# A decoder layer's way into its expert stage: the first two searches, the samples' mixing and four weight loads set in another order

## What is computed

```python
x = x + (ga * ya + gb * yb) @ w_out
x = x + peer(rmsnorm(x, norm_ffn), peer_wq, peer_keys, peer_u, peer_v)

def peer(tb, wq, keys, u, v):                      # 8 heads, 128 keys in each half
    q = (tb @ wq).reshape(blk, 8, 256)
    s1 = einsum('thd,hkd->thk', q[..., :128], keys[:, 0])
    s2 = einsum('thd,hkd->thk', q[..., 128:], keys[:, 1])
    sc1, i1 = top_k(s1, 16)
    sc2, i2 = top_k(s2, 16)
    cand = sc1[..., :, None] + sc2[..., None, :]   # 16 x 16 sums
    sc, sel = top_k(cand, 16)                      # 16 experts of 16384
    idx = (i1 * 128 + i2) at sel
    g = softmax(sc)
    act = gelu(einsum('thkd,td->thk', u[idx], tb))
    return einsum('thk,thkd->td', g * act, v[idx])
```

## Time and profile before

| | us |
|---|---|
| median of 3 runs | 2117.23 |
| lowest, highest | 2110.43, 2120.0 |
| profiled execution | 2117.6 |
| its span, first to last instruction | 2116.1 |
| its mean granted TensorE clock | 0.824 |
| TensorE matmul, VectorE, ScalarE, GpSimd busy | 1670.0, 1447.7, 489.1, 667.8 |
| transfers | 749.11 MB, mean 354 GB/s |
| gathers | 528, median 12.8 from issue to landing |

### The profile page before, as it was taken

One profiled execution on the slowest core, in us unless ns is written; L12 is line 12 of the kernel. 1 busy time (PEld: TensorE's weight loads), 2 busy tenths in 40 slices (PEclk: granted clock), 3 DMA queues, 4 the chain that ended last, 5 costly groups with the idle time before them and its releaser, 6 DMA issues. The chain is left out here.

```text
span 2116.1 us, 30101 instructions
## 1 busy us (share of the span) xinstructions
PE 1670.0 (79%) x10874; PEld 842.1 (40%) x10874; DVE 1447.7 (68%) x3666; ACT 489.1 (23%) x1413; POOL 667.8 (32%) x614
## 2 busy tenths in 40 slices
PE   7999999877777666666789999997777866666666
PEld 6887677433333111111168786773332421111111
DVE  3557533778778878877726575347877878887786
ACT  2246211211121221111223553122121112111112
POOL 0011000444554454444300110004454444444442
PEclk9999999877897676665799999999787876666658
DMA  5458895999999999999854688969999999999997
GB/s 205 157 204 305 300 389 229 387 370 420 416 421 421 404 416 420 421 415 414 366 181 150 218 318 297 387 240 408 404 421 420 416 420 402 421 421 420 416 413 304
DMA packets 135936, 749.11 MB, mean 354 GB/s; under 512 B 16611, under 2 KB 17100, under 8 KB 57298
## 3 DMA queue, kind: packets, MB, share of 16 engines
q0 software_dynamic: 84640, 588.54, 68.2%
q1 hardware_dynamic: 51138, 158.55, 20.6%
HBM read 735.70 MB, written 11.52 MB: 353 GB/s over the span
## 5 line engine op out<-in xcount | busy, mean ns | idle before, releaser
L1221 PE MATMUL ps<-arena 64*64 64x512 f32 x4096 | 753.2, 836 | 384.0 <-DVE arena L1841 381.7
L2463 POOL DMA_INDIRECT arena<-in_peer_uv,arena x528 | 619.9, 1174 | 792.2 <-PE ps L1221 642.7
L1832 DVE CUSTOM_DVE_ANT_0 arena<-arena,h 128x1024 f32<-128x1024 f32 x512 | 627.3, 1225 | 241.3 <-DMA arena<-in_peer_uv,arena 235.4
L1221 PEld LDWEIGHTS ps<-arena 64*64 64x64 f32 x4096 | 141.1, 166 | 938.6 <-DVE arena L1841 889.7
L573 PE MATMUL ps<-ht_tok,wring 128*128 128x264 f32 (+1 forms) x1536 | 362.9, 395 | 4.5 <-DMA wring<-in_w_in 3.1
L2204 ACT ACTIVATE arena<-arena 128x1 f32<-128x1 f32 x528 | 105.4, 203 | 975.1 <-DVE arena L1832 974.0
L573 PEld LDWEIGHTS ps<-ht_tok,wring 128*128 128x128 f32 x1536 | 292.8, 194 | 75.6 <-issue 19.9
L1841 DVE TENSOR_SCALAR arena<-consts,arena 128x64 f32<-128x64 f32 (+1 forms) x528 | 164.6, 312 | 25.2 <-ACT arena L2204 24.6
L573 PE MATMUL ps<-arena,wring 128*128 128x264 f32 x256 | 64.1, 393 | 2.7 <-DVE arena L1536 2.7
L573 PE MATMUL ps<-arena,gate 128*128 128x256 f32 x256 | 59.0, 382 | 0.0
L2440 POOL DMA_DIRECT2D nrow<-in_norm_ffn x2 | 1.1, 536 | 174.2 <-PE ps L925 174.2
(11 more groups left out here) (374 smaller groups left out, 1791.3 us busy)
## 6 DMA issues: line engine op xcount, KB each, us to landing
arena<-in_pages SPq DMA_DIRECT2D x256, 272.0 KB, 6.1
wring<-in_w_in SPq DMA_DIRECT2D x36, 1024.0 KB, 5.0
arena<-in_peer_uv,arena POOLq DMA_INDIRECT x528, 12.8
h<-in_state_ssm POOLq DMA_DIRECT2D x16, 512.0 KB, 6.1
out<-h POOLq DMA_DIRECT2D x16, 512.0 KB, 6.3
wring<-in_w_ssm_proj SPq DMA_DIRECT2D x8, 1024.0 KB, 10.8
arena<-in_w_out SPq DMA_DIRECT2D x8, 1024.0 KB, 9.4
wring<-in_peer_wq SPq DMA_DIRECT2D x8, 1024.0 KB, 9.7
```

Of the source, the lines that this page charges most:

```text
L1221: last = pe.matmul(ps[to:to + 64, SUM_BANK[t] + i, :], diag[rows, n % DIAGS, 0:64], ring[rows, HOME[n % RING], cols], start=n in TILE_FIRS ...
L1832: dve.tensor_tensor_reduce(ring[:, HOME[k], 0:D_MODEL], ring[:, HOME[k], 0:D_MODEL], tokens, 1.0, 0.0, ALU.mult, ALU.add, dots[:, column(n ...
L2463: pool.indirect_dma_start(ring[:, HOME[k], :], None, table, bass.IndirectOffsetOnAxis(ap=idx[:, TOPK * u + j:TOPK * u + j + 1], axis=0)).t ...
```

## The change

- TensorE's order: the four products of tile 0 come first; the samples' mixing and its turns stand behind the fourth, among the turns of tile 0's normed rows; `sample_heads`, `sample_mla_parts` and `sample_mla` stand behind scores 0; queries and scores of head 1 stand behind `out(3, 1)`, directly ahead of the outputs.
- Norm of tile 0 in parts: ScalarE squares each quarter when it is added, and the rows are scaled in two halves, each of which is turned by itself. The first query product starts on the first half.
- Corner search: for heads 0 and 1 of tile 0 the first eight numbers are searched among the 8 x 8 sums of the best eight of either half, the second eight among all 16 x 16. Both hand over eight numbers at a time. No piece of head 1's search stands ahead of the slots; in slots 5 to 8 four pieces run each.
- Tiles 1 and 2: squares, root and norm two slots later; TensorE's turns behind outputs 8, 9 and 10, head 2's products behind 12 and 13, its scores behind 14 as before.
- Loads: heads 0, 3 and 4 when the newest sample's scores are made, head 2 into the rear half of `gate` when tile 0 and 1 are mixed, heads 1, 5 and 6 behind `sample_mla_parts`, head 7 as before. To make the room of head 0's block free early, ScalarE copies the samples' latents aside. Rooms in the arena are in another order, and the rows of `peer_wq` are laid so that the turns read contiguous columns.

```diff
     for first in range(3):
-        steps[7 + first] = [("rows", first)]
+        steps[8 + first] = [("rows", first)]
...
-        at = (2, 6, 10) if hh > 2 else (11, 12, 14)
+        at = (2, 6, 10) if hh > 2 else (12, 13, 14)
...
+                    def first_rows(q):
+
+                        pe.wait_ge(sem("ph_ready"), q + 1)
+                        b = aux.fill()
+                        for c in range(4 * q, 4 * q + 4):
+                            last = turn(ps[:, b, (c % 4) * P:(c % 4 + 1) * P], rows_of(0, c), P)
+                        aux.filled(last)
+                        marks["turned", 0] = aux.n
...
+                    out(3, 0)
+                    samples_mixed()
+                    first_rows(0)
+                    samples_turned()
+                    first_rows(1)
                     queries(0, 0, 0, P)
                     queries(0, 1, 0, P)
                     scores(0, (0,))
-                    queries(1, 0, 0, P)
+                    sample_heads()
+                    sample_mla_parts()
+                    out(0, 1)
                     sample_mla()
-                    queries(1, 1, 0, P)
-                    out(0, 1)
-                    scores(1, (0,))
                     out(1, 1)
...
                     out(3, 1)
                     marks["x", 1] = aux.n
+                    queries(1, 0, 0, P)
+                    queries(1, 1, 0, P)
+                    scores(1, (0,))
...
+                    def first_experts(u):
+
+                        dve.wait_ge(sem("scores_out"), SCORES_AT[u, 0])
+                        halves = [keysc[:, u, 0, half, :] for half in range(2)]
+                        for k in range(2):
+                            at = [slice(TOPK * half + 8 * k, TOPK * half + 8 * k + 8) for half in range(2)]
+                            for half in range(2):
+                                last = dve.max(top[:, at[half]], halves[half])
...
+                            width = 8 * (k + 1)
+                            sums = cand[:, 0:width * width]
+                            then(dve.tensor_tensor(sums.rearrange("p (i j) -> p i j", i=width), bc(top[:, 0:width], 2, width),
+                                                   bc(top[:, TOPK:TOPK + width], 1, width), ALU.add))
+                            yield
...
+                            then(dve.max(ctop[:, eight], sums))
+                            then(dve.max_index(ctopi[:, eight], ctop[:, eight], sums))
+                            yield
+                            yield from expert_numbers(u, k, width)
...
-                    ahead = best_experts(1)
-                    for _ in range(10):
-                        next(ahead)
...
+                    ahead = first_experts(1)
...
-                        for _ in range(0 if n < 4 else 3):
+                        for _ in range(0 if n < 5 else 4 if n < 9 else 3):
                             next(ahead, None)
...
-                        elif n == 6:
+                        elif n == 8:
                             px_rows((1, 2))
...
+                    sp.wait_ge(sem("aux_full"), marks["newest_scored"])
+                    sp.dma_start(wq_latents, w_q[0]).then_inc(sem("latents_load"), 16)
+                    sp.dma_start(wq_early, w_q[3]).then_inc(sem("early_load"), 16)
                     sp.dma_start(wq_home, w_q[4]).then_inc(sem("home_load"), 16)
...
+                    sp.wait_ge(sem("mixed"), 1)
+                    sp.dma_start(wq_gates, w_q[2]).then_inc(sem("early_load"), 16)
```

More of the change, by code:

```diff
@@ L482, in build @@
         wq_early = by_chunk(peer("wq_early"))
+        wq_gates = gate[:, DC:, 0:BLOCK]
         diag = peer("diag").rearrange("p (k d) -> p k d", k=DIAGS)
@@ L2154, in _ @@
                     wide.emptied(act.copy(ols[:, 1, :, :].rearrange("p h (j g) -> p j g h", j=2), turned[:, :, 1, :, 0:A_HEADS]))
-                    act.wait_ge(sem("aux_free"), 4 + marks["x", 0])
-                    squares(hp[0], x[:, 0, :], st[:, 45:46], "px0_squares")
-                    root(st[:, 48:49], st[:, 45:46], "px0")
-                    b = wide.read()
-                    wide.emptied(act.copy(ot[:, :, SEQ:TOKENS], ps[:, b, 0:4 * SAMPLES].rearrange("p (q b) -> p q b", q=4)))
-                    for half in range(2):
-                        b = wide.read()
-                        wide.emptied(act.copy(mla_parts[:, half * 512:(half + 1) * 512], ps[:, b, :]))
                     scored = [0]
@@ L2208, in _ @@
                     scores_out(0, (0,))
-                    queries_out(1, 0, 0, P)
-                    queries_out(1, 1, 0, P)
-                    scores_out(1, (0,))
+                    b = wide.read()
+                    wide.emptied(act.copy(ot[:, :, SEQ:TOKENS], ps[:, b, 0:4 * SAMPLES].rearrange("p (q b) -> p q b", q=4)))
+                    for half in range(2):
+                        b = wide.read()
+                        wide.emptied(act.copy(mla_parts[:, half * 512:(half + 1) * 512], ps[:, b, :]))
                     exponents(0)
                     def late_tiles(n):
-                        if n == 4:
+                        if n == 6:
                             act.wait_ge(sem("aux_free"), 4 + marks["x", 1])
```

223 lines of the change are left out of this document (140 added, 83 removed).

## The result

The changed kernel takes 2135.8 us (median of 5 runs, 2132.1 to 2139.4). The kernel before took 2117.2 in the same comparison. The ratio is 1.0086, 95% interval 1.006 to 1.0112: slower, where 2120 and "no difference" were forecast; the time lies above the range of 2108 to 2129. The profiled execution has 2132.1 us and a span of 2130.5, against 2117.6 and 2116.1, so 14.4 us more are to be found in the trace, not the 2.3 of the sum.

What follows compares the result with a forecast made beforehand. The bound was taken to be the chain from the norm of tiles 1 and 2 through turns and head 2's products to head 2's search. Terms 0.7 + 0.7 + 0.9 = +2.3 us on 2117.6 gave 2120 us, range 2108 to 2129.

Steps and rivals of the forecast that it cites:

- the sum: Forecast total: 0.7 + 0.7 + 0.9 = +2.3 us on the profiled execution's 2117.6, giving 2119.9.
- The bound and its place: Chain of norm of tiles 1 and 2, turns, head 2's products and search; its end sets the time.
- The gate: VectorE's MAX8 that begins head 2's search, at 428.95 and 1474.76 before; forecast +0.7 us in each layer.
- Up to the first search: From the first output product to head 0's scores on VectorE: 355.0 in place of 362.93, 7.9 us earlier.
- The search: Head 0's first eight numbers on VectorE: 3.8 us in place of 6.7, first gather 10.8 us earlier.
- Heads 1, 5 and 6 beside gathers 0 to 3: Weight loads at 359.5 beside the first gathers: seven transfers, 17.4 us, done about 378; cost 0.
- VectorE's cost: Head 1's search pieces and dot products ahead of the norm of tiles 1 and 2: norm ends 403.4, 4.3 us later.
- The clock, from the last output ahead of the turns to the gate: Turns 1.6 to 2.5 us later; 24.8 and 20.3 us to the gate, less one output; 0.9 in the total.
- The rival "the half clock lasts": TensorE's pauses in the rounds of four search pieces keep its clock low: slower, 2124 to 2130; chance 0.20.
- Lead carried: Rival: transfers bind from the start, so the gathers' lead reaches the end, 5.9 us per layer, 2105.8; chance 0.12.
- VectorE catches up: Rival: search pieces slip into VectorE's waits, TensorE's 2.9 us lead reaches the gate in each layer, 2111.8; chance 0.18.

Runs made afterwards that it cites:

- experiment 3: Norm of tiles 1 and 2 two slots earlier in the changed kernel: 2121.3 us, ratio 1.0024; two slots later in the kernel before: 2128.0 us, 1.0042.
- experiment 6: Changed kernel with filler transposes that nobody reads in TensorE's waits ahead of the turns: 2134.6 us, ratio 1.0087; with more of them 2127.3 us, 1.0057.
- experiment 7: Head 2's search from slot 18, not 16: changed kernel 2126.1 us, 1.0043; with the edits of experiments 1 to 3, 0.9954; kernel before 2114.4 us, 0.9984.
- experiment 1: Changed kernel with later loads of heads 1, 5 and 6: 2129.3 us, 1.0063; or with copies of the samples' sums one slot earlier: 2128.0 us, 1.0051.
- experiment 2: Changed kernel with eight diagonals of 64 columns in place of four of 128: 2133.8 us, ratio 1.0087.
- the filler: Transposes that nobody reads, added to the changed kernel in TensorE's waits ahead of the turns (experiment 6); the longer version took 2127.3 us, ratio 1.0057.
- experiment 4: Kernel before with the corner search for head 0 alone: 2116.0 us, ratio 0.9985.
- the later search: Head 2's search from slot 18 in place of 16 (experiment 7): changed kernel 2126.1 us, ratio 1.0043; kernel before 2114.4 us, 0.9984.
- the last kernel: The kernel of experiment 8, the changed kernel with several edits, later search of head 2 and filler transposes: 2106.6 us, ratio 0.9929.
- experiment 8: Changed kernel with the edits of experiments 1 to 3, head 2's search from slot 18, and 42 and 14 filler transposes: 2106.6 us, ratio 0.9929.

## Why the forecast was wrong

**The bound and its place: right.** The gate moved with the time in all kernels, in that of experiment 3 (both directions) as in that of experiment 6. Gather 40 follows it by 45 to 48 us wherever the search starts at slot 16, and the time of the profiled execution less the start of layer 1's gate is 642.2 to 644.3 us in all thirteen kernels with that start. The gate is a bound and no bystander: two dot products moved ahead of it shorten the time (experiment 7).

**Up to the first search: right within 1 us.** Fourth product's end 346.85 for 346.2, query product 350.88 for 350.2, MAX8 355.97 for 355.0. 0.65 of it lies ahead of the seam, where the mix already is at 330.86 in place of 330.21.

**The search: right.** Numbers 3.9 us behind the first MAX8 for 3.8; first gather 360.12 for 359.1. Layer 1's first gather came at 1416.4 and not 1409.5, since it carries layer 0's delay (last gather 1047.8 for 1041.4).

**Heads 1, 5 and 6 beside gathers 0 to 3, priced at 0: the step that failed first.** I counted when all seven transfers were done and who reads the eighth gather, not when gather 1 lands and what stands on VectorE behind its dot product: the copies that TensorE's halves wait for. It costs 3.9 us in layer 0 and 2.0 in layer 1 of this trace (experiment 1), in other traces up to 5; against the forecast only 2.8 and 0.95, since the other products there came out 1 us shorter than counted. The Trainium skill ("Trainium Kernel Development and Optimization", "Key Constraints") says that transfers issued from several queues run on the same 16 engines and interleave; by that rule the three blocks slow the gathers just behind them, and the trace agrees: without them dot product 1 began 5.5 us earlier.

**VectorE's cost: the right step, mis-sized.** First output to norm's end is 18.3 for 17.4. The 0.9 is a wait that I had not listed: the diagonal of slot 4 needs output 0 (experiment 2). The norm ends at 408.0 and not at 403.4: 2.8 of that from the first output, 0.9 from this wait, 1.0 from the start of the search. The pieces themselves cost what the working said, and experiment 3 shows that the norm's place is worth 13 us in the two layers.

**The clock, from the last output ahead of the turns to the gate: the step that failed by most.** The sum has 0.9 for it; no run shows such a term. The traces show, against the forecast, 1.8 in layer 0, and 0.9 ahead of the turns and 3.9 behind them in layer 1, 6.6 in all. Of the 3.9 the filler gives back 3.0 (23.2 to 20.2, at a granted clock of 1.00); the other 0.85 is no clock but TensorE's wait of 1.31 us for a diagonal, by which the output that I had counted as saved saves nothing. I had read the 20.3 of one trace's layer 1 as a property of the kernel. It is one of two values that the same instructions take from execution to execution (experiment 4), and in the changed kernel and its variants with these turns and no filler the slow one came in all ten layers traced. The rival "the half clock lasts" was right in mechanism, and the forecast gave it 0.20; it lacked the terms above. The Trainium skill ("TensorE: Matmul & The Clock Gate", "What's actually happening") says that the low clock is the default and that activity lifts it; the filler bears this out (0.50 without it, 1.00 with it).

**In sum:** layer 0's gate is late by 1.0 (start) + 2.8 (first output) + 0.9 (diagonal) + 1.8 (clock) = 6.5 us; layer 1 adds 0.95 + 0.9 + 0.9 + 3.9 = 6.7, less the 0.9 that the sum had for the clock: 12.3 in all, against 12.2 between 2119.9 and 2132.1. This is the account of one execution, the fastest of five; the median is 3.7 above it, and no trace shows where those lie.

**The other rivals.** *Lead carried* fell: a nearer first gather alone hardly moved the turns (experiment 4), and ten microseconds at the first gather were gone by gather 8 (391.7 for 390.8). *VectorE catches up* fell: the slack was real, as experiment 7 shows, but only moving dot products into it uses it.

Open: why the later search gains more than two dot products, what tips the clock in one execution and not in the next, and whether its fall in layer 1 of the last kernel can be kept off.

## What to carry to other kernels

A transfer with slack for its own reader is not free: ask which gather lands beside it, which instruction waits for that, and what stands behind that instruction in its engine's program. When a change makes engines wait more often, price TensorE's half clock in every layer, and waits for free buffers with those for data. Before you forecast from a stretch that differs between two layers or two traces, look at more traces: it may be a matter of the execution and not of the kernel. Where an engine waits for its next input with other inputs landed, move ready work ahead of the wait; that was one line, and took 0.0043 off the changed kernel's ratio and 0.0016 off that of the kernel before.

## What the runs showed of the hardware beyond that

- The granted clock also reacts to work without a reader: 128x128 fp32 transposes kept it at 1.00 where it was 0.50 (experiment 6). Back to back one takes 0.11 us (44 in 5.02), about twice that in the slow stretch of experiment 8.
- The same instructions can keep or lose the clock at the same place, in the two layers of one execution (24.8 and 20.3 us before) and in two executions (layer 0's 412 to 416: 0.50 before, 1.00 in the kernel of experiment 7 that differs from it only behind that place; and the four matmuls behind a wait of some 3 us, 1.88 or up to 3.58 us). A microsecond moved ahead of such a place may bring four or none.
